# A two-layer trunk on one core: the MLP's down projection as seven block products, with block sums on GpSimd

## The chip, the cores and the metric

One core of a Trainium2 chip runs the whole kernel. The time is that of the device, in microseconds (us), from one launch; lower is better. Engines: TensorE (PE; its weight loads are PEld), VectorE (DVE), ScalarE (ACT), GpSimd (POOL), SyncE (SP), which here only issues DMAs.

## The reference

Two layers over x of 512 tokens by 1024 features, all in float32. Each layer has a token mixer (dilated attention, a gating unit and retention, between an input and an output projection), cross-attention into 256 memory tokens, and an MLP; each of the three has a norm before it and one behind it. Cut to the MLP, and to what is around it:

```python
for l in range(DEPTH):
    ...
    mem_n = rms_norm(mem, g[6])
    x = x + rms_norm(memory_attention(rms_norm(x, g[2]), mem_n, x_wq[l], x_wkv[l], x_wo[l]), g[3])
    h = rms_norm(x, g[4])
    f = jnp.square(jax.nn.relu(h @ w_up[l])) @ w_down[l]     # (512,1024)@(1024,4096), (512,4096)@(4096,1024)
    x = x + rms_norm(f, g[5])
```

## The kernel before

Every float32 product is made of three matmuls in the type fp32r: each operand is split into a high part, rounded, and a low part, the remainder, and hi·hi, hi·lo and lo·hi are summed in PSUM (`three_passes`, L558 to L560). Weights come in blocks of 512 rows by 512 columns, in SBUF as 128 partitions x 2048. A block goes through four steps: SyncE loads it into one of two slots of `w_raw`, ScalarE writes `w_hi` (`split_hi`, L934), VectorE writes `w_lo` = `w_raw` - `w_hi` (`split_lo`, L1193), TensorE uses it. `w_hi` and `w_lo` have two slots as well, so ScalarE may split block b only when TensorE is done with b-2 (semaphore `tile_done`), and SyncE may load only when the slot's block is split (`w_lo_done`).

A layer has 36 head blocks (JOBS), and then the MLP in four groups of 1024 hidden features. A group has eight blocks: `up0`, `up1` (each two blocks of 512 input features) and `dn0`, `dn1` (each two blocks of 512 hidden features). TensorE runs a block as four tiles of 12 matmuls (4 slices of 128 by 3 passes), one tile to each of the four PSUM banks of `proj`. Behind an up tile ScalarE makes the relu (L1114) and the high part `uT_hi` (L1117), VectorE the square (L1487) and the low part `uT_lo` (L1491). Behind the second block of a down job VectorE adds each bank to `ys` (L1500). `ys` was zeroed by GpSimd before (L1644), which does nothing else in the MLP until the norm at the end of the layer.

The order of every engine is written out by hand, each in its own program of straight code and `Fori` loops: an instruction that waits holds up everything behind it on its engine. Around the MLP:

- The third norm (`n3`), between the output of cross-attention and the first up blocks, has its order in two lists, `N3_ACT` and `N3_DVE`. In them e is a tile's square sum or gain, x the updated row tile and its squares, n the norm, h the split of its transposes (L961, L1254), w the split of up block 0 or 1.
- In the last group of a layer the sums of squares of `ys`, the gains (L1238) and the updates of `xs` (L1246) follow the additions of `dn1`, tile by tile; GpSimd takes the roots (L1577, L1579). In layer 0 the memory for the next layer is normed and transposed in the same group, and the next layer's first weight block is loaded when it ends.
- The prologue: SyncE loads positions, a table, the memory tokens `hs`, the gains, the first weight block and x; VectorE makes the angles of the rotary positions (11 small steps); ScalarE loads its sine table, makes sine and cosine, loads the exponential's table (L922 to L925), and only then squares the memory tokens (L1122). GpSimd makes the root, VectorE the norm (L1224), TensorE transposes (L587), and both split the transposes (`memT_hi`, `memT_lo`).

## Time and profile before

| | us |
|---|---|
| median of 3 runs (1556.33 to 1559.43) | 1556.99 |
| the profiled execution, whole | 1556.43 |
| its span (first to last instruction of the trace) | 1554.4 |
| TensorE busy, 8016 matmuls | 1519.2 |
| VectorE busy | 735.9 |
| ScalarE busy | 572.5 |
| GpSimd busy | 177.2 |

The profiled execution's own time is 2.0 us longer than its span. Busy time is the time in which an engine had an instruction in work; matmuls overlap each other in the pipeline, so their mean durations (0.39 us) are longer than the distance from one to the next. The granted clock of TensorE is 0.998 of full over the span. Reading such a profile starts from the engine that is never idle; what the others do counts only where it ends a wait of that one.

### The profile page before, as it was taken

Reading aid. Unit: us, or ns where it says so; the run is one execution under the profiler, and the core shown is the slowest. Engines: PE = TensorE matmul, PEld = TensorE weight load, DVE = VectorE, ACT = ScalarE, POOL = GpSimd, SP = SyncE. Lnnn points to the kernel's source line nnn. Section 1 sums busy time; section 2 is a strip of 40 time slices with the busy share of each in tenths; the row PEclk is TensorE's granted clock in tenths of the full one; section 3 lists DMA queues with packets and bytes.
Section 4 is the critical chain, followed back from the end, with each engine's and each line's share of the span. In section 5 each row is a group of like instructions: output and inputs, shape, how many; then the busy total and the mean of one; then the engine's idle time right before and its main releaser. Section 6 shows DMA issues by size and latency. Waiting matters only on the chain.

```text
span 1554.4 us, 19807 instructions
## 1 busy us (share of the span) xinstructions
PE 1519.2 (98%) x8016; PEld 1302.3 (84%) x8016; DVE 735.9 (47%) x933; ACT 572.5 (37%) x865; POOL 177.2 (11%) x192
## 2 busy tenths in 40 slices
PE   5999999999999999999999999999999999999997
PEld 5978898888888888888898888888888888888886
DVE  5345555724554343433572465755346433444345
ACT  5335434534443232313352453344334423232231
POOL 2001710200110000000040037111003000000001
PEclk9999999999999999999999999999999999999999
DMA  7333132430223332333343232125112232323231
GB/s 248 117 101 102 42 109 82 163 109 28 60 84 106 105 99 91 97 126 115 109 130 115 64 106 91 66 82 175 70 49 88 82 98 92 108 82 108 83 121 55
DMA packets 78991, 153.62 MB, mean 99 GB/s; under 512 B 3520, under 2 KB 19648, under 8 KB 78912
## 3 DMA queue, kind: packets, MB, share of 16 engines
q1 hardware_dynamic: 77904, 150.50, 29.4%
...
q14 instruction: 21, 0.17, 0.0%
...
## 4 chain that ended last, share of the span: by engine, by line
PE 94%; DVE 3%; ACT 1%; issue 1%; POOL 1%; DMA 1%; POOLq 0%; ACTq 0%; SPq 0%; DVEq 0%
PE proj L558 28%; PE proj L560 27%; PE proj L559 27%; PE work L758 2%; PE work L587 2%; PE work L737 2%; PE work L623 1%; PE work L634 1%; PE work L613 1%; DVE w_lo L1193 1%; PE work L712 1%; ACT w_hi L934 0%; DMA w_raw<-in_x_wkv_dram 0%; PE work L691 0%; PE work L745 0%
## 5 line engine op out<-in xcount | busy, mean ns | idle before, releaser
L1193 DVE TENSOR_TENSOR w_lo<-w_raw,w_hi 128x2048 fp32r<-128x2048 f32 (+1 forms) x136 | 297.3, 2186 | 463.7 <-ACT w_hi L934 463.6
L934 ACT ACTIVATE w_hi<-w_raw 128x2048 fp32r<-128x2048 f32 (+1 forms) x136 | 248.2, 1825 | 475.2 <-PE proj L560 469.9
L558 PE MATMUL proj<-hT_hi,w_hi 128*128 128x512 f32 (+1 forms) x800 | 299.3, 374 | 4.3 <-DVE w_lo L1193 4.3
L559 PE MATMUL proj<-hT_lo,w_hi 128*128 128x512 f32 (+1 forms) x800 | 298.2, 373 | 0.0
L560 PE MATMUL proj<-hT_hi,w_lo 128*128 128x512 f32 (+1 forms) x800 | 298.2, 373 | 0.0
L558 PE MATMUL proj<-w_hi,hT_hi 128*128 128x512 f32 (+1 forms) x640 | 238.4, 372 | 1.2 <-DVE hT_lo L1298 1.2
L560 PE MATMUL proj<-w_hi,hT_lo 128*128 128x512 f32 (+1 forms) x640 | 232.2, 363 | 0.0
L559 PE MATMUL proj<-w_lo,hT_hi 128*128 128x512 f32 (+1 forms) x640 | 231.8, 362 | 0.0
L558 PE MATMUL proj<-w_hi,uT_hi 128*128 128x512 f32 x512 | 199.4, 389 | 0.0
L560 PE MATMUL proj<-w_hi,uT_lo 128*128 128x512 f32 x512 | 199.2, 389 | 0.0
L559 PE MATMUL proj<-w_lo,uT_hi 128*128 128x512 f32 x512 | 199.2, 389 | 0.0
L558 PEld LDWEIGHTS proj<-hT_hi,w_hi 128*128 128x128 f32 x800 | 151.2, 189 | 30.9 <-DVE w_lo L1193 4.7
L559 PEld LDWEIGHTS proj<-hT_lo,w_hi 128*128 128x128 f32 x800 | 151.2, 189 | 26.2
L560 PEld LDWEIGHTS proj<-hT_hi,w_lo 128*128 128x128 f32 x800 | 151.2, 189 | 26.0
L558 PEld LDWEIGHTS proj<-w_hi,hT_hi 128*128 128x128 f32 x640 | 120.6, 188 | 13.8 <-DVE hT_lo L1298 1.7
L560 PEld LDWEIGHTS proj<-w_hi,hT_lo 128*128 128x128 f32 x640 | 120.1, 188 | 13.0
L559 PEld LDWEIGHTS proj<-w_lo,hT_hi 128*128 128x128 f32 x640 | 120.4, 188 | 11.8
L559 PEld LDWEIGHTS proj<-w_lo,uT_hi 128*128 128x128 f32 x512 | 96.1, 188 | 20.0
L560 PEld LDWEIGHTS proj<-w_hi,uT_lo 128*128 128x128 f32 x512 | 96.1, 188 | 19.9
L558 PEld LDWEIGHTS proj<-w_hi,uT_hi 128*128 128x128 f32 x512 | 96.1, 188 | 19.9
L1571 POOL TENSOR_SCALAR half_mean<-half_sum 128x4 f32<-128x4 f32 x6 | 1.4, 233 | 908.1 <-ACT half_squares L948 908.1
L1500 DVE TENSOR_TENSOR ys<-proj,ys 128x512 f32<-128x512 f32 x64 | 44.0, 689 | 70.9 <-PE proj L560 70.7
...
## 6 DMA issues: line engine op xcount, KB each, us to landing
w_raw<-in_w_up_dram SPq DMA_DIRECT2D x32, 1024.0 KB, 5.8
w_raw<-in_w_down_dram SPq DMA_DIRECT2D x32, 1024.0 KB, 5.1
...
w_raw<-in_x_wkv_dram SPq DMA_DIRECT2D x16, 1024.0 KB, 5.1
w_raw<-in_w_out_dram SPq DMA_DIRECT2D x8, 1024.0 KB, 5.2
w_raw<-in_x_wq_dram SPq DMA_DIRECT2D x8, 1024.0 KB, 5.1
w_raw<-in_x_wo_dram SPq DMA_DIRECT2D x8, 1024.0 KB, 5.1
gains<-in_norm_g_dram SPq DMA_DIRECT2D x13, 512.0 KB, 6.2
```

The source lines that it names most:

```text
L558: nc.tensor.matmul(dst, l_hi, r_hi, start=first, stop=False)
L559: nc.tensor.matmul(dst, l_hi, r_lo, start=False, stop=False)
L560: return nc.tensor.matmul(dst, l_lo, r_hi, start=False, stop=last)
L587: mm = nc.tensor.transpose(work[:, 2 * (n % 2) + half, k * P:(k + 1) * P], src[:, c * P:(c + 1) * P], ident[:])
L613: mm = nc.tensor.matmul(work[:, head, 0:n], left[rows, p, q], right[rows, p, 0:n], start=i == 0, stop=i == len(passes) - 1)
L623: mm = nc.tensor.transpose(work[:, 2, j * P:(j + 1) * P], probs[:, u % 2, j * P:(j + 1) * P], ident[:])
L634: mm = nc.tensor.matmul(work[HD * head:HD * (head + 1), 3, p * P:(p + 1) * P], va[:, j, (h + head) * HD:(h + head + 1) * HD], probsT[:, he ...
L737: mm = nc.tensor.matmul(work[:, u % 2, i * MEM:(i + 1) * MEM], qxT[:, c, t * P:(t + 1) * P], kmT[:, c, :], start=(k == 0), stop=(k == 1))
L758: mm = nc.tensor.matmul(work[:, 3, k * P:(k + 1) * P], vm[:, j, (pair * BK + k) * P:(pair * BK + k + 1) * P], x_probsT[:, u % 2, (i * MT + ...
L934: nc.scalar.activation(w_hi[:, slot, :, 0:cols], w_raw[:, slot, :, 0:cols], ACT.Copy).then_inc(w_hi_done, 1)
L1193: nc.vector.tensor_tensor(w_lo[:, slot, :, 0:cols], w_raw[:, slot, :, 0:cols], w_hi[:, slot, :, 0:cols].bitcast(F32), ALU.subtract).then_i ...
L1500: nc.vector.tensor_tensor(part_y, proj[:, t], part_y, ALU.add).then_inc(added, 1)
```

## The change

The down projection of a group is a product of A, 512 tokens by 1024 hidden features, and B, 1024 by 1024. Both are cut in four: a11, a12, a21, a22 (first or second 256 tokens, first or second 512 hidden features) and b11 to b22. In place of the eight block products there are seven (Winograd's form of Strassen's scheme), each of 256 tokens by one block of 128x2048, 24 matmuls, on operands that are in part sums:

| product | rows | weights |
|---|---|---|
| m1 | a11 | b11 |
| m2 | a12 | b21 |
| m6 | a21 + a22 - a11 | b22 - b12 + b11 |
| m5 | s1 = a21 + a22 | b12 - b11 |
| m7 | s3 = a11 - a21 | t3 = b22 - b12 |
| m3 | a12 - (a21 + a22 - a11) | b22 |
| m4 | a22 | b21 - (b22 - b12 + b11) |

GpSimd makes the sums in place: four of weights (128x2048 each), s3 (128x1024), s1 and the new a11 in two halves each (128x512), and the new a12 (128x1024). ScalarE and VectorE split the rows of each product (128x1024, three slots `a_hi`, `a_lo`) and its weights (128x2048, the two slots as before). m1, m6, m7 and m4 run in PSUM banks 2 and 3 and stay there as a running sum, m2, m5 and m3 in banks 0 and 1, m3 on top of m5; after every product VectorE adds its two banks to a quarter of `ys` (in the first group it copies four of the seven). The relu is written once to `u` and squared there in place; the split of the up tiles (`uT_hi`, `uT_lo`) is gone, as are the zeroing of `ys` and the loops: each group is written out. Two of four down blocks, b12 and b22, are loaded into new slots (`w_more`) ahead of their group; the bytes loaded are the same.

Beside that: the third norm splits up block 1 before row tile 2 or 3 is squared or updated; the next layer's first two weight blocks are loaded and split in the last group, where only one was; the prologue loads the memory first, in separate semaphores by tile, its gains by ScalarE's queue, the first weight block in halves, and two weight blocks instead of one, and it makes the angles, sine and cosine behind the splits of the memory's transposes.

In the diff below, blank lines and these parts are left out: the new names and semaphores, `load_up` and `load_down`, `product_hi` and `rows_hi` (a split that waits for its operand's sum and for the slot), `add_product`, and what only follows from these.

```diff
-GROUP_JOBS = ("up0", "up1", "dn0", "dn1")
-GROUP_BLOCKS = KB * len(GROUP_JOBS)
+UP_BLOCKS = 2 * KB
+PRODUCTS = ("m1", "m2", "m6", "m5", "m7", "m3", "m4")
+GROUP_BLOCKS = UP_BLOCKS + len(PRODUCTS)
 BLOCKS = HEAD_BLOCKS + GROUPS * GROUP_BLOCKS
+RAW_GROUP = UP_BLOCKS + 2
+RAWS = HEAD_BLOCKS + GROUPS * RAW_GROUP
+ADDS = 2 * len(PRODUCTS)
+ASLOTS = 3
...
-N3_ACT = steps("e0 e1 x0 x1 w0 h0 e2 h1 x2 e3 w1 x3 h2 h3")
-N3_DVE = steps("e0 x0 e1 x1 n0 n1 w0 h0 h1 e2 x2 e3 x3 w1 n2 n3 h2 h3")
+N3_ACT = steps("e0 e1 x0 x1 w0 h0 e2 h1 e3 w1 x2 x3 h2 h3")
+N3_DVE = steps("e0 x0 e1 x1 n0 n1 w0 h0 h1 e2 x2 e3 w1 x3 n2 n3 h2 h3")
...
+        u = part("u", 0, [P, KC, S])
+        s1 = part("s1", 16, [P, BK, S // 2])
+        a_hi = part("a_hi", 20, [P, ASLOTS, BK, S // 2], F32R)
+        a_lo = part("a_lo", 20 + 4 * ASLOTS, [P, ASLOTS, BK, S // 2], F32R)
+        w_more = part("w_more", 44, [P, 3, BK, 512])
+        s3 = nc.alloc_sbuf_tensor_at("s3", [P, BK, S // 2], F32, offset=sgu_start)
+        a11, a21 = u[:, 0:BK, 0:S // 2], u[:, 0:BK, S // 2:S]
+        a12, a22 = u[:, BK:KC, 0:S // 2], u[:, BK:KC, S // 2:S]
+        ROWS = {"m1": a11, "m2": a12, "m6": a11, "m5": s1[:], "m7": s3[:], "m3": a12, "m4": a22}
+        RAW = {"m1": w_raw[:, 0], "m2": w_raw[:, 1], "m6": w_raw[:, 0], "m5": w_more[:, 1], "m7": w_more[:, 2],
+               "m3": w_more[:, 0], "m4": w_raw[:, 1]}
...
+            def free_raws(l, g):
+                sp.wait_ge(w_lo_done, nth(w_lo_done, l, product_block(g, "m6") + 1))
+                sp.wait_ge(t_made, nth(t_made, l, 4 * g + 4))
+            def load_group(l, g):
+                if g:
+                    free_raws(l, g - 1)
+                    load_up(l, g, 0)
+                    sp.wait_ge(w_lo_done, nth(w_lo_done, l, product_block(g - 1, "m5") + 1))
+                    load_down(l, g, w_more[:, 1], 0, 1, q_loaded[1])
+                    sp.wait_ge(w_lo_done, nth(w_lo_done, l, product_block(g - 1, "m3") + 1))
+                    load_down(l, g, w_more[:, 0], 1, 1, q_loaded[0])
+                    sp.wait_ge(w_lo_done, nth(w_lo_done, l, product_block(g - 1, "m4") + 1))
+                    load_up(l, g, 1)
+                else:
+                    for i in range(KB):
+                        sp.wait_ge(w_lo_done, nth(w_lo_done, l, HEAD_BLOCKS - WSLOTS + i + 1))
+                        load_up(l, g, i)
+                    sp.wait_ge(x_weighed, nth(x_weighed, l, XUNITS))
+                    load_down(l, g, w_more[:, 1], 0, 1, q_loaded[1])
+                    load_down(l, g, w_more[:, 0], 1, 1, q_loaded[0])
+                for i in range(KB):
+                    sp.wait_ge(w_lo_done, nth(w_lo_done, l, group_block(g, i) + 1))
+                    load_up(l, g, KB + i)
+                for i in range(KB):
+                    sp.wait_ge(w_lo_done, nth(w_lo_done, l, group_block(g, KB + i) + 1))
+                    load_down(l, g, w_raw[:, i], i, 0, w_loaded[i])
...
-            for dst, src in ((pos_i, positions), (inv, c_inv)):
-                sp.dma_start(dst[:], src).then_inc(first_loaded, 16)
             for t in range(MT):
-                sp.dma_start(hs[:, t], mem[0, t * P:(t + 1) * P]).then_inc(mem_loaded, 16)
-            load_gain(0, "mem")
-            load_block(PROLOGUE, BLOCKS, x_wkv[0:1, 0:BK * P, 0:512])
-            for t in range(T):
+                sp.dma_start(hs[:, t], mem[0, t * P:(t + 1) * P]).then_inc(mem_first[t], 16)
+            for h in range(2):
+                k = BK // 2 * h
+                sp.dma_start(w_raw[:, 0, k:k + BK // 2],
+                             x_wkv[0, k * P:(k + BK // 2) * P, 0:512].rearrange("(k p) c -> p k c", p=P)).then_inc(w_first[h], 16)
+            load_block(PROLOGUE, BLOCKS + 1, x_wkv[0:1, BK * P:2 * BK * P, 0:512])
+            sp.dma_start(xs[:, 0], x[0, 0:P]).then_inc(x_loaded[0], 16)
+            load_gain(0, "n1")
+            for t in range(1, T):
                 sp.dma_start(xs[:, t], x[0, t * P:(t + 1) * P]).then_inc(x_loaded[t], 16)
+            start_counts(sp, mem_loaded)
+            sp.sem_inc(w_loaded[0], 16)
...
+            def product(l, g, name):
+                n = PRODUCTS.index(name)
+                b = product_block(g, name)
+                a = (len(PRODUCTS) * g + n) % ASLOTS
+                bank = 2 if name in ("m1", "m6", "m7", "m4") else 0
+                fresh = name in ("m1", "m2", "m5")
+                pe.wait_ge(w_lo_done, nth(w_lo_done, l, b + 1))
+                pe.wait_ge(a_lo_done, nth(a_lo_done, l, len(PRODUCTS) * g + n + 1))
+                for i in range(2):
+                    if name == "m1":
+                        pe.wait_ge(relued, nth(relued, l, UP_TILES * g + 6 + i + 1))
+                    elif n >= 2:
+                        pe.wait_ge(added, nth(added, l, ADDS * g + 2 * (n - 2) + i + 1))
+                    rows = slice(i * P, (i + 1) * P)
+                    for k in range(BK):
+                        mm = three_passes(proj[:, bank + i], a_hi[:, a, k, rows], a_lo[:, a, k, rows],
+                                          w_hi[:, b % WSLOTS, k], w_lo[:, b % WSLOTS, k],
+                                          fresh and k == 0, k == BK - 1, more=True)
+                    mm.then_inc(tile_done, 1)
+                    if name == "m3" and g == GROUPS - 1 and l < DEPTH - 1:
+                        turn_normed(l, "memk", i)
...
+            def mlp_group(l, g):
+                last = g == GROUPS - 1
+                if g:
+                    split_hi(l, group_block(g, 1))
+                split_hi(l, group_block(g, 2))
+                if last and l < DEPTH - 1:
+                    act.wait_ge(turned, nth(turned, l, 2 * TURNED["n3", T - 1] + 2))
+                    for t in range(MT):
+                        act.dma_start(hs[:, t], mem[0, t * P:(t + 1) * P]).then_inc(mem_loaded, 16)
+                    act.dma_start(gains[:, GAIN_SLOT["mem"]],
+                                  norm_g[l + 1:l + 2, GAIN["mem"]].broadcast_to([P, D])).then_inc(gain_loaded["mem"], 16)
+                for m in range(4):
+                    relu_up(l, g, m)
+                split_hi(l, group_block(g, 3))
+                rows_hi(l, g, "m1")
+                product_hi(l, g, "m1")
+                for m in range(4, 8):
+                    relu_up(l, g, m)
+                product_hi(l, g, "m2")
+                rows_hi(l, g, "m2")
+                rows_hi(l, g, "m6")
+                product_hi(l, g, "m6")
+                rows_hi(l, g, "m5")
+                product_hi(l, g, "m5")
+                rows_hi(l, g, "m7")
+                if last:
+                    e3_squares(l, 0, (0, 1))
+                product_hi(l, g, "m7")
+                rows_hi(l, g, "m3")
+                product_hi(l, g, "m3")
+                rows_hi(l, g, "m4")
+                product_hi(l, g, "m4")
+                if not last:
+                    split_hi(l, group_block(g + 1, 0))
+                    return
+                e3_squares(l, 0, (2, 3))
+                if l < DEPTH - 1:
+                    split_hi(l, BLOCKS)
+                    for t in range(MT):
+                        turn_hi(l, ("memk", t), memT_hi, t)
+                e3_squares(l, 1, (0, 1))
+                if l < DEPTH - 1:
+                    split_hi(l, BLOCKS + 1)
+                e3_squares(l, 1, (2, 3))
...
+            def mlp_group(l, g):
+                last = g == GROUPS - 1
+                if g:
+                    split_lo(l, group_block(g, 1))
+                split_lo(l, group_block(g, 2))
+                for m in range(4):
+                    square_up(l, g, m)
+                split_lo(l, group_block(g, 3))
+                rows_lo(l, g, "m1")
+                if last and l < DEPTH - 1:
+                    for t in range(MT):
+                        norm_mem(l, "memk", t)
+                product_lo(l, g, "m1")
+                for m in range(4, 8):
+                    square_up(l, g, m)
+                product_lo(l, g, "m2")
+                rows_lo(l, g, "m2")
+                for n, name in enumerate(PRODUCTS[:-2]):
+                    add_product(l, g, name, 0)
+                    add_product(l, g, name, 1)
+                    rows_lo(l, g, PRODUCTS[n + 2])
+                    product_lo(l, g, PRODUCTS[n + 2])
+                add_product(l, g, "m3", 0)
+                if last:
+                    gain(l, "e3", 0, 0)
+                    gain(l, "e3", 0, 1)
+                add_product(l, g, "m3", 1)
+                if not last:
+                    split_lo(l, group_block(g + 1, 0))
+                    add_product(l, g, "m4", 0)
+                    add_product(l, g, "m4", 1)
+                    return
+                if l < DEPTH - 1:
+                    split_lo(l, BLOCKS)
+                    for t in range(MT):
+                        turn_lo(l, ("memk", t), memT_hi, memT_lo, t)
+                gain(l, "e3", 0, 2)
+                gain(l, "e3", 0, 3)
+                gain(l, "e3", 1, 0)
+                update(l, "e3", 0)
+                add_product(l, g, "m4", 0)
+                add_product(l, g, "m4", 1)
+                if l < DEPTH - 1:
+                    split_lo(l, BLOCKS + 1)
+                gain(l, "e3", 1, 1)
+                update(l, "e3", 1)
+                for t in (2, 3):
+                    gain(l, "e3", 1, t)
+                    update(l, "e3", t)
...
+            def mlp_group(l, g):
+                b11, b21 = w_raw[:, 0], w_raw[:, 1]
+                b22, b12, t3 = w_more[:, 0], w_more[:, 1], w_more[:, 2]
+                def rows_read(name):
+                    pool.wait_ge(a_lo_done, nth(a_lo_done, l, len(PRODUCTS) * g + PRODUCTS.index(name) + 1))
+                for q in q_loaded:
+                    pool.wait_ge(q, nth(q, l, 16 * (g + 1)))
+                if g:
+                    pool.wait_ge(w_lo_done, nth(w_lo_done, l, product_block(g - 1, "m7") + 1))
+                else:
+                    pool.wait_ge(x_weighed, nth(x_weighed, l, XUNITS))
+                nc.gpsimd.tensor_tensor(t3, b22, b12, ALU.subtract).then_inc(t_made, 1)
+                r = HEAD_BLOCKS + RAW_GROUP * g + UP_BLOCKS
+                pool.wait_ge(w_loaded[0], nth(w_loaded[0], l, 16 * (r // WSLOTS + 1)))
+                pool.wait_ge(t_made, nth(t_made, l, 4 * g + 1))
+                nc.gpsimd.tensor_tensor(b12, b12, b11, ALU.subtract).then_inc(t_made, 1)
+                pool.wait_ge(hidden, nth(hidden, l, UP_TILES * g + BK))
+                if g:
+                    pool.wait_ge(a_lo_done, nth(a_lo_done, l, len(PRODUCTS) * (g - 1) + PRODUCTS.index("m7") + 1))
+                nc.gpsimd.tensor_tensor(s3[:], a11, a21, ALU.subtract).then_inc(s_made, 1)
+                pool.wait_ge(w_lo_done, nth(w_lo_done, l, product_block(g, "m1") + 1))
+                pool.wait_ge(t_made, nth(t_made, l, 4 * g + 2))
+                nc.gpsimd.tensor_tensor(b11, t3, b11, ALU.add).then_inc(t_made, 1)
+                rows_read("m1")
+                for half in range(2):
+                    k = slice(half * 2, half * 2 + 2)
+                    pool.wait_ge(hidden, nth(hidden, l, UP_TILES * g + BK + half * 2 + 2))
+                    nc.gpsimd.tensor_tensor(s1[:, k], a21[:, k], a22[:, k], ALU.add).then_inc(s_made, 1)
+                    pool.wait_ge(s_made, nth(s_made, l, 6 * g + 2 * half + 2))
+                    nc.gpsimd.tensor_tensor(a11[:, k], s1[:, k], a11[:, k], ALU.subtract).then_inc(s_made, 1)
+                pool.wait_ge(w_lo_done, nth(w_lo_done, l, product_block(g, "m2") + 1))
+                pool.wait_ge(t_made, nth(t_made, l, 4 * g + 3))
+                nc.gpsimd.tensor_tensor(b21, b21, b11, ALU.subtract).then_inc(t_made, 1)
+                rows_read("m2")
+                pool.wait_ge(s_made, nth(s_made, l, 6 * g + 5))
+                nc.gpsimd.tensor_tensor(a12, a12, a11, ALU.subtract).then_inc(s_made, 1)
...
-                nc.gpsimd.memset(ys[:], 0.0).then_inc(y_zeroed, 1)
+                for g in range(GROUPS):
+                    mlp_group(l, g)
```

## Rows read from the trace of the kernel before

**Rows 1.** the page: busy time, and the chain that ended last
```profile
PE 1519.2 (98%) x8016; PEld 1302.3 (84%) x8016; DVE 735.9 (47%) x933; ACT 572.5 (37%) x865; POOL 177.2 (11%) x192
...
PE 94%; DVE 3%; ACT 1%; issue 1%; POOL 1%; DMA 1%; POOLq 0%; ACTq 0%; SPq 0%; DVEq 0%
```

**Rows 2.** TensorE's waits: us in total, times, longest us
```profile
PE work L587 <- DVE hs L1224: 13.9, 1, 13.9
PE proj L558 <- DVE w_lo L1193: 7.6, 4, 2.2
```

**Rows 3.** windows, one middle group (busy PE, PEld, DVE, ACT, POOL)
```profile
578.85:665.89 87.04, 87.04 (x386) 72.07 (x385) 34.04 (x33) 24.27 (x24) 0.00 (x0) 1.00 0.30 97
```

**Rows 4.** timeline of an up block: start us, us, engine, line, operation
```profile
533.70 0.39 PE L558 MATMUL proj<-hT_hi,w_hi 128*128 128x512 f32 x1
...
533.98 0.60 ACT L1114 ACTIVATE relu<-proj 128x512 f32<-128x512 f32 x1 [0.89 <-PE proj L560]
...
537.33 0.69 DVE L1487 TENSOR_TENSOR relu<-relu 128x512 f32<-128x512 f32 x1 [1.31 <-ACT relu L1114]
```

**Rows 5.** the line of w_lo (ns min/median/max), then groups by form (mean ns)
```profile
L1193 DVE TENSOR_TENSOR w_lo<-w_raw,w_hi x136: 1757/2291/2294, 14.9 to 1527.8; 128x2048 fp32r<-128x2048 f32 x108, 128x1536 fp32r<-128x1536 f32 x28
...
L1209 DVE SCALAR_TENSOR_TENSOR hs<-xs,rstd,gains 128x1024 f32<-128x1024 f32 x24 | 30.8, 1283 | 8.7 <-POOL rstd L1566 8.7
...
L934 ACT ACTIVATE w_hi<-w_raw 128x2048 fp32r<-128x2048 f32 x108 | 206.6, 1913 | 436.9 <-PE proj L560 431.7 <-DMA w_raw<-in_x_wkv_dram 5.1
```

**Rows 6.** groups by form, GpSimd
```profile
L1594 POOL TENSOR_TENSOR qkc<-rot 128x384 f32<-128x384 f32 x8 | 8.3, 1039 | 0.6
...
L1619 POOL TENSOR_TENSOR vs<-vs,ln_gain 128x1024 f32<-128x1024 f32 x2 | 4.8, 2400 | 12.2 <-DVE vs L1313 12.2
```

**Rows 7.** timeline, GpSimd beside VectorE, two places
```profile
141.83 2.37 POOL L1621 TENSOR_TENSOR vs<-vs,ln_shift 128x1024 f32<-128x1024 f32 x1
...
142.00 2.35 DVE L1262 TENSOR_SCALAR probs<-probs,rden 128x256 f32<-128x256 f32 x1
...
938.60 1.08 POOL L1594 TENSOR_TENSOR qkc<-rot 128x384 f32<-128x384 f32 x1
939.64 2.53 POOL L1595 TENSOR_TENSOR qkc<-qkc,rot 128x384 f32<-128x384 f32 x1
...
939.23 2.06 DVE L1193 TENSOR_TENSOR w_lo<-w_raw,w_hi 128x1536 fp32r<-128x1536 f32 x1 [0.42 <-ACT w_hi L934]
```

**Rows 8.** timeline, a handover near the kernel's end
```profile
1547.70 1.28 DVE L1246 SCALAR_TENSOR_TENSOR xs<-ys,rstd,xs 128x1024 f32<-128x1024 f32 x1
1548.90 0.68 DVE L1238 TENSOR_TENSOR ys<-ys,gains 128x512 f32<-128x512 f32 x1
...
1547.83 1.20 POOL L1577 TENSOR_TENSOR meansq<-sumsq,half_mean 128x1 f32<-128x1 f32 x1 [0.89 <-ACT squares L954]
```

**Rows 9.** DMA issues: engine op xcount, KB each, us to landing
```profile
w_raw<-in_w_down_dram SPq DMA_DIRECT2D x32, 1024.0 KB, 5.1
...
gains<-in_norm_g_dram SPq DMA_DIRECT2D x13, 512.0 KB, 6.2
```

**Rows 10.** timeline of the prologue, and the last update
```profile
9.07 1.04 ACT L1122 ACTIVATE squares<-hs 128x1024 bf16<-128x1024 f32 x1
11.59 1.91 ACT L934 ACTIVATE w_hi<-w_raw 128x2048 fp32r<-128x2048 f32 x1 [0.35 <-DMA w_raw<-in_x_wkv_dram]
...
12.47 2.48 DVE L1224 SCALAR_TENSOR_TENSOR hs<-hs,mem_rstd,gains 128x1024 f32<-128x1024 f32 x2 [5.42 <-POOL mem_rstd L1604]
...
19.59 0.39 PE L558 MATMUL proj<-memT_hi,w_hi 128*128 128x256 f32 x1 [2.05 <-DVE memT_lo L1254]
...
1550.03 1.28 DVE L1246 SCALAR_TENSOR_TENSOR xs<-ys,rstd,xs 128x1024 f32<-128x1024 f32 x1 [0.44 <-POOL rstd L1579]
```

**Rows 11.** window behind the first pause, and eight later transposes on the timeline
```profile
13.90:15.00 1.10, 1.10 (x6) 1.10 (x7) 1.10 (x2) 0.00 (x0) 0.00 (x0) 1.00 1.04 413
...
437.23 1.03 PE L587 MATMUL work<-ident,hs 128*128 128x128 f32 x8
```

415 lines of the change are left out of this document (215 added, 200 removed).

## The prediction, made before the changed kernel ran

> **What bounds the kernel now.** I read the page first: TensorE is busy for 98% of the span, and the chain that ended last is TensorE for 94% [rows 1]. The list of waits then shows how little can be won by waiting less: TensorE waits 13.9 us once at the start and 7.6 us in four waits for w_lo; these two lines lead the list [rows 2]. One middle MLP group of eight blocks, by windows, takes 87.04 us with TensorE busy throughout, VectorE for 34.0 us, GpSimd not at all [rows 3]: a block of 48 matmuls lasts 10.88 us, a tile of 12 lasts 2.72 us. So the MLP is bound by the number of matmuls, and everything the change adds to other engines is free until it makes TensorE wait. The timeline gives the delays: ScalarE starts 0.28 us after the next tile's first matmul; a relu lasts 0.60 us, a square 0.69 us [rows 4].
>
> **What goes.** A group has four down blocks of 48 matmuls; afterwards it has seven products of 24. 24 matmuls fewer are 5.44 us, over 8 groups **-43.5 us**. A group without waits would last 81.6 us. The memset of ys (GpSimd, unwaited for) goes at no gain.
>
> **What comes.** Each product still needs a whole split of a 128x2048 block (ScalarE 1.91, VectorE 2.29 us by the median) [rows 5], but TensorE spends only 5.44 us on it, and with two slots the split may start only when the product two before is done. VectorE has per product that split, a 128x1024 remainder (1.28 us by the nearest row; between the 512 and 2048 forms it would be 1.2, which I take) and two additions of 0.69: 4.9 of 5.44 us. ScalarE has 1.91 + 1.05 (the 128x1024 form, [rows 10]). That fits, barely, if nothing else holds VectorE up.
>
> GpSimd comes in per group with four sums of 128x2048 and the equal of four of 128x1024. It has a two-input 1024 form at 2.40 us and a 384 form at 1.04 [rows 6]: 2.13 ns an element, so 4.6, 2.4 and 1.27 us for 2048, 1024 and 512. There is no row of 2048; in proportion to the 1024 form it would be 4.8, so I take 4.2 to 5.0 as ends. The walk below holds two such sums in series: 0.8 us of wait a group either way, 6 us in all.
> The Trainium skill (GPSIMD Engine Reference, Elementwise — side-by-side cycle accounting) has 4497 ns for a two-input sum of 2048; by it the time would be about 2 us less.
>
> **The port.** A VectorE subtraction with both inputs in SBUF began beside a GpSimd operation and lasted 2.06 us, where its form, the shorter on that line, takes 1.76 at the least [rows 5, 7]; the next GpSimd operation of 384 elements lasted 2.53 us instead of 1.0, that is, until the subtraction had ended. A VectorE scaling of 256 elements begun 0.17 us into a 2.37 us GpSimd operation lasted 2.35 us [rows 7]. So each waits for the other's whole instruction. When both are ready at the end of an instruction the one that waited longer goes first: GpSimd's small sum of 1547.83 ended 0.13 us after the next VectorE instruction's start, not behind it [rows 8]. By these rows a handover comes 0.14 us ahead of the record's end.
> The Trainium skill says the same (SBUF — State Buffer, Who interferes with whom): a VectorE instruction with two SBUF inputs and a GpSimd one that reads SBUF exclude each other for a whole instruction. It speaks against this change, and the trace agrees.
>
> **One group on that port**, in us from the start of m1 on TensorE (the end of the last up block):
> - w_lo of m1 until -6.4, square 4 until -5.8; then the sum into b11, -6.0 to -1.3. Squares 5 and 6, ready at -4.5 and -1.9, wait: done -0.8 and -0.2.
> - First halves of the two row sums and square 7, in turn: -0.3 to 1.0, 0.9 to 1.6, 1.5 to 2.8.
> - w_hi of m2 comes behind relu 7 (0.9 to 2.7), w_lo 2.7 to 5.0; the second s1 half, waiting, takes 4.9 to 6.2, the remainder of m2's rows 6.0 to 7.25. m1 ended at 5.44: **wait 1.85 us**; m2 ends 12.7.
> - Second a11 half 7.1 to 8.4; from it ScalarE makes m6's rows until 9.5. But GpSimd is free at once for the 4.6 us sum into b21 (8.5 to 13.1), needed only by the last product. Behind it m6's row remainder 13.0 to 14.1, then, waiting longer, the sum into a12 until 16.4, then w_lo of m6 until 18.55. m6 starts 18.6 instead of 12.7: **wait 5.85 us**.
> - From there VectorE's 4.9 us fit into each 5.44.
>
> That is 7.7 us a group, **+61.6 us**. At six seams between groups the next t3 sum (its data issued after m3's split, 5.1 us to landing [rows 9]) ends about 0.2 us too late for the first up block's w_lo: +1.2. The sum into b12, s3 and their loads lie in the up phase, where a block lasts 10.88 us and its split 4.2; 4.6 us more still fit, so they cost nothing.
>
> **The rest.** Prologue: ScalarE sits behind sine and exponential tables until 9.07, the norm starts at 12.47, the first product at 19.59 [rows 10]. Memory is now loaded first, the tables come later, and the gains are issued near 1.0 on ScalarE's queue; with the 6.2 us to landing of such a load [rows 9] the norm starts near 7.2. The first weight block, whose load ended at 11.59, is issued 1.5 us earlier and in halves: near 10. Its two small splits and the four remainders of memT (0.6 each) then end near 14.5: -5.0, and one of the four w_lo waits (1.9 in the mean) goes: **-6.9** (ends -3 and -8.5). Behind it the eleven trigonometric steps, 3 us on VectorE, stand before the second split; the first block's 5.7 us cover them, without that cover they'd cost 3. Third norm: two waits of up to 2.2 us for w_lo go, the transposes' remainders are late next, so I take half of 2 x 2.2: **-2.2**. Layer seam: the w_lo wait goes, but VectorE now puts one split, four remainders, three gains and an update (some 9 us) ahead of the last product's additions, on whose banks the next block waits: 0 (ends -1.9, +2). Tail: m4's additions stand behind one update of 1.28 and gains; the last update, 1550.03 now [rows 10], ends later by **+1.6** (ends 0, +3).
>
> **Sum**: -43.5 +61.6 +1.2 -6.9 -2.2 +1.6 = +11.8 on the profiled execution's 1556.4 us (span 1554.4): 1568.2; against the runs' median of 1557.0, 0.6 higher, **1569**. The wait per group at which the change earns nothing is 49.8 / 8 = 6.2 us. A measurement tells 0.2%, 3 us, from no change.
>
> **Rivals.**
> - *VectorE keeps the port* over instructions that follow one another. Then the waits are 0.7 and 4.95, 5.65 in all, and the time 1552. Rows 8 speak against it; its rows are of tiny sums.
> - *The port's queue is shorter* than I walked it: if the sum into b11 ends before square 5 is ready, the second a11 half ends at 4.3, not 8.4, and about 2.7 us a group are left: 1529, **faster**. For it: each start hangs on margins of 0.1 to 0.5 us. Against: the sum can't start before w_lo of m1.
> - *No exclusion for subtractions*: rows 7 have only 0.30 us of it on one. Then 0.7 us a group: 1512.
> - *The clock*. After the first 13.9 us pause six transposes stand in 1.10 us, 0.18 each; later eight stand in 1.03, 0.13 each, though the granted clock reads 1.00, the 2.4 GHz level, in both [rows 11]. If the product behind each 5.85 us pause runs slower, at most 5.44 us, at half that 2.7 a group: 1591. Against: the granted clock, and that each product is followed at once by three or more without a pause.
> The Trainium skill (TensorE: Matmul & The Clock Gate, Rules for kernel authors) says that idle gaps of this length bring the half rate back; no row here shows a granted clock below 1.00.
> - *It doesn't do what it says*: 192 matmuls remain, 1600. Nothing speaks for it.
>
> **Chances.** As walked 0.42 (own range 1558 to 1580), VectorE keeps the port 0.14, shorter queue 0.18, no exclusion 0.12, clock 0.12, not as it says 0.02. Faster: 0.18 + 0.12 + 0.08 of the 0.14 = 0.38; same 0.05; slower 0.57. The range takes in the shorter queue and most of the clock's case, 1524 to 1592; no exclusion stays outside.
>
> **What would show it.** TensorE waiting in every group for m2's row remainder (about 1.9 us) and m6's w_lo (about 5.9), and nowhere else in the MLP; L1193-like subtractions of over 4 us beside GpSimd's sums; GpSimd busy 28 us a group or more; the first matmul before 10 us. Wrong, if those subtractions all last 2.29 us, if waits per group are under 6.2 us, or if the 2048 sums last well under 4.2.

## The result, and the profile after

The changed kernel takes 1606.41 us (median of 4 runs, 1605.50 to 1607.57) against 1556.66 for the kernel before (4 runs, 1555.93 to 1559.43): a ratio of 1.0317, 95% interval 1.0299 to 1.0334. It is slower, as forecast, but by 50 us and not by 12, and it lies 14 us above the range of 1524 to 1592. Its span is 1604.1 us.

The page of the profile, busy time and chain, as in [rows 1]:
```profile
PE 1506.9 (94%) x7824; PEld 1283.3 (80%) x7824; DVE 971.9 (61%) x998; ACT 636.5 (40%) x883; POOL 453.7 (28%) x272
...
PE 81%; DVE 9%; POOL 5%; ACT 2%; issue 2%; DMA 1%; SPq 0%; DVEq 0%; POOLq 0%; ACTq 0%
```
The 192 matmuls are gone, and TensorE is busy 12 us less, not 43.5: matmuls became longer. It now idles for 6% of the span. Its waits (us in total, times, longest):
```profile
PE proj L647 <- DVE w_lo L1333: 43.0, 8, 5.4
PE proj L647 <- DVE a_lo L1340: 13.6, 8, 1.7
PE work L676 <- DVE hs L1378: 12.8, 5, 4.0
PE work L676 <- DMA ident<-in_c_ident_dram: 9.0, 1, 9.0
```
The first two lines are one wait ahead of m6 and one ahead of m2 in each of the eight groups. The third is new too: two in each layer's third norm, one at the layer seam. What makes m6 late is seen in one middle group on the timeline, GpSimd first, then VectorE, then TensorE:
```profile
578.03 4.65 POOL L1831 TENSOR_TENSOR w_raw<-w_raw 128x2048 f32<-128x2048 f32 x1
582.61 3.36 POOL L1835 TENSOR_TENSOR u<-u 128x1024 f32<-128x1024 f32 x1
...
579.20 4.56 DVE L1340 TENSOR_TENSOR a_lo<-u,a_hi 128x1024 fp32r<-128x1024 f32 x1 [1.08 <-ACT a_hi L1058]
583.68 4.43 DVE L1333 TENSOR_TENSOR w_lo<-w_raw,w_hi 128x2048 fp32r<-128x2048 f32 x1
...
577.07 0.47 PE L647 MATMUL proj<-w_hi,a_hi 128*128 128x512 f32 x1 [1.70 <-DVE a_lo L1340]
588.17 0.80 PE L647 MATMUL proj<-w_hi,a_hi 128*128 128x512 f32 x1 [5.41 <-DVE w_lo L1333]
588.76 0.63 PE L648 MATMUL proj<-w_lo,a_hi 128*128 128x512 f32 x1
589.19 0.63 PE L649 MATMUL proj<-w_hi,a_lo 128*128 128x512 f32 x1
...
593.43 0.40 PE L647 MATMUL proj<-w_hi,a_hi 128*128 128x512 f32 x1
593.67 0.40 PE L648 MATMUL proj<-w_lo,a_hi 128*128 128x512 f32 x1
```
The sum for m4 (L1831), needed last of all, holds m6's row remainder up until 582.7; the remainder's record, 4.56 us for 1.2 us of work, is mostly waiting. Then the sum for m3 (L1835) holds up the remainder of m6's weights. That is the walk of the forecast to within half a microsecond. What it did not have is in the last lines: from 588.17 on matmuls start 0.43 us apart in place of 0.23, until 593.4. The windows of that stretch (the third figure from the end is the granted clock), the group's 26 us ahead of the pause among them:
```profile
556.00:582.00 26.00, 24.30 (x108) 19.85 (x107) 18.00 (x11) 10.87 (x10) 18.05 (x7) 1.00 0.10 38
588.00:593.00 5.00, 4.83 (x11) 3.80 (x12) 4.65 (x5) 0.00 (x0) 0.00 (x0) 0.50 0.65 209
546.75:638.85 92.10, 84.84 (x362) 69.02 (x360) 62.51 (x41) 32.39 (x26) 35.26 (x11) 0.96 0.28 92
```
Granted clock 0.50, the 1.2 GHz level, behind the pause of 5.41 us; 1.00 behind m2's of 1.70. The twelve distances from 588.17 to 593.43 take 5.26 us; the same twelve behind m2's wait take 2.81. That is 2.45 us in this group. Over the eight groups, ten to twelve matmuls are slow each time. The whole group, from one sum into b12 to the next, takes 92.10 us where [rows 3] had 87.04.

**Where the 49.7 us of span are.** I took the same instruction in both traces at six places; what the shift gains between two of them belongs to that stretch:

| stretch | forecast | found |
|---|---|---|
| prologue (first kmT, 31.82 and 28.08) | -6.9 | -3.7 |
| third norm (first relu of the MLP, 451.05 and 452.08; in layer 1 1215.94 and 1244.92) | -2.2 | +7.3 (4.8 and 2.5; in layer 1 the kernel before lost some itself) |
| eight groups | +19.3 | +39.5 |
| layer seam | 0 | +5.0 |
| behind the last matmul (1545.88 and 1594.00, ends of span) | +1.6 | +1.6 |
| sum | +11.8 | +49.7 |

The third norm in layer 0, GpSimd, VectorE and TensorE:
```profile
432.46 4.55 POOL L1806 TENSOR_TENSOR w_more<-w_more 128x2048 f32<-128x2048 f32 x1
...
432.53 5.56 DVE L1378 SCALAR_TENSOR_TENSOR hs<-xs,rstd,gains 128x1024 f32<-128x1024 f32 x1 [0.72 <-PE work L676]
...
438.15 1.97 PE L676 MATMUL work<-ident,hs 128*128 128x128 f32 x8 [3.76 <-DVE hs L1378]
```
GpSimd's first block sum t3 starts 0.07 us ahead of the last norm, which then lasts 5.56 us in place of 1.28. TensorE waits 3.76 us and runs its next transposes slowly (granted clock 0.66 from 436 to 446). Layer 1 has the same wait, at 1231.73.

### The profile page after: what moved, and what is told of

Its sections match the earlier page's. It is cut to its first block, busy times and chain, and to the rows that moved or that the text cites. A ratio compares the mean times of both kernels' runs of the same rounds, so it can differ in the third digit from the quotient of the medians.

```text
span 1604.1 us, 19050 instructions
## 1 busy us (share of the span) xinstructions
PE 1506.9 (94%) x7824; PEld 1283.3 (80%) x7824; DVE 971.9 (61%) x998; ACT 636.5 (40%) x883; POOL 453.7 (28%) x272
## 4 chain that ended last, share of the span: by engine, by line
PE 81%; DVE 9%; POOL 5%; ACT 2%; issue 2%; DMA 1%; SPq 0%; DVEq 0%; POOLq 0%; ACTq 0%
PE proj L647 23%; PE proj L649 23%; PE proj L648 23%; POOL s L1825 2%; DVE w_lo L1333 2%; DVE u L1346 2%; POOL u L1827 2%; PE work L676 2%; PE work L847 2%; DVE w_lo L1326 2%; PE work L826 2%; PE work L712 1%; PE work L723 1%; ACT w_hi L1032 1%; PE work L702 1%
## 5 line engine op out<-in xcount | busy, mean ns | idle before, releaser
L1326 DVE TENSOR_TENSOR w_lo<-w_raw,w_hi 128x2048 fp32r<-128x2048 f32 (+1 forms) x103 | 229.0, 2224 | 287.6 <-ACT w_hi L1032 287.3
L1032 ACT ACTIVATE w_hi<-w_raw 128x2048 fp32r<-128x2048 f32 (+1 forms) x103 | 185.1, 1797 | 245.7 <-PE proj L649 244.7
L647 PE MATMUL proj<-w_hi,a_hi 128*128 128x512 f32 x448 | 184.1, 411 | 56.6 <-DVE w_lo L1333 43.0
L648 PE MATMUL proj<-w_lo,a_hi 128*128 128x512 f32 x448 | 181.6, 405 | 0.0
L649 PE MATMUL proj<-w_hi,a_lo 128*128 128x512 f32 x448 | 181.1, 404 | 0.0
L647 PEld LDWEIGHTS proj<-w_hi,a_hi 128*128 128x128 f32 x448 | 89.0, 199 | 81.8 <-DVE w_lo L1333 46.4
L648 PEld LDWEIGHTS proj<-w_lo,hT_hi 128*128 128x128 f32 x640 | 120.4, 188 | 11.8
L1346 DVE TENSOR_TENSOR u<-u 128x512 f32<-128x512 f32 x64 | 84.1, 1329 | 49.2 <-ACT u L1223 49.2
L1340 DVE TENSOR_TENSOR a_lo<-u,a_hi 128x1024 fp32r<-128x1024 f32 x40 | 106.0, 2651 | 8.6 <-ACT a_hi L1058 8.6
L1333 DVE TENSOR_TENSOR w_lo<-w_raw,w_hi 128x2048 fp32r<-128x2048 f32 x32 | 90.5, 2828 | 33.7 <-ACT w_hi L1046 33.7
L649 PEld LDWEIGHTS proj<-w_hi,a_lo 128*128 128x128 f32 x448 | 88.4, 197 | 19.4
```

The source lines that it names most:

```text
L647: nc.tensor.matmul(dst, l_hi, r_hi, start=first, stop=False, skip_group_check=more)
L648: nc.tensor.matmul(dst, l_hi, r_lo, start=False, stop=False, skip_group_check=more)
L649: return nc.tensor.matmul(dst, l_lo, r_hi, start=False, stop=last, skip_group_check=more)
L1032: nc.scalar.activation(w_hi[:, slot, :, 0:cols], w_raw[:, raw, :, 0:cols], ACT.Copy).then_inc(w_hi_done, 1)
L1326: nc.vector.tensor_tensor(w_lo[:, slot, :, 0:cols], w_raw[:, raw, :, 0:cols], w_hi[:, slot, :, 0:cols].bitcast(F32), ALU.subtract).then_in ...
L1333: nc.vector.tensor_tensor(w_lo[:, b % WSLOTS], RAW[name], w_hi[:, b % WSLOTS].bitcast(F32), ALU.subtract).then_inc(w_lo_done, 1)
```

## Experiments

Two theories to start with. *Port and order*: TensorE waits because VectorE's instructions with two SBUF inputs and GpSimd's sums exclude each other, and the two sums L1831 and L1835 come at the worst moment; then the half clock behind the pause. *Engine time*: GpSimd or the chain through it is simply too slow, whatever VectorE does. Runs e1 to e4 are single runs, beside 1556.16 for the kernel before; e5 to e7 stand beside a median of 1556.77, e8 to e10 beside 1556.41. A span is that of the one profiled execution and can lie 2 us from the span of the median run, so small differences are read from the medians.

**e1: both late sums only behind m6's split.**
```diff
-                pool.wait_ge(w_lo_done, nth(w_lo_done, l, product_block(g, "m2") + 1))
+                pool.wait_ge(w_lo_done, nth(w_lo_done, l, product_block(g, "m6") + 1))
+                rows_read("m2")
+                nc.gpsimd.tensor_tensor(a12, a12, a11, ALU.subtract).then_inc(s_made, 1)
                 nc.gpsimd.tensor_tensor(b21, b21, b11, ALU.subtract).then_inc(t_made, 1)
-                rows_read("m2")
-                nc.gpsimd.tensor_tensor(a12, a12, a11, ALU.subtract).then_inc(s_made, 1)
```


> Edit: GpSimd makes the a12 sum and then the b21 sum only behind m6's w_lo, instead of ahead of it. Theory (port and clock: a GpSimd sum holds the port that VectorE's subtractions need, and a pause of over 5 us halves TensorE's rate behind it): the wait for m6's w_lo falls from 5.4 to about 1 us a group, but VectorE has only 0.5 us free per product, so the 7 us of sums now stand before m5's or m7's w_lo and some 5 us of wait a group appear there; time 1575 to 1606. Rival (VectorE is simply full, GpSimd is not the cause): the wait stays before m6, time unchanged at 1606. Rival (m6's operands are late because the GpSimd chain itself is long): wait at m6 gone, none elsewhere, 1545.

1603.33 us, span 1601.5. TensorE's waits in one middle group (556 to 648):
```profile
PE proj L647 <- DVE w_lo L1333: 4.9, 2, 4.4
PE proj L647 <- DVE a_lo L1340: 1.7, 1, 1.7
```
and on VectorE in that group:
```profile
584.78 6.65 DVE L1333 TENSOR_TENSOR w_lo<-w_more,w_hi 128x2048 fp32r<-128x2048 f32 x1
```
The pause moved from m6 to m5 (0.56 and 4.38 us in place of 5.41), with half the rate behind it as before, and the time is inside the 1575 to 1606 expected. Delaying whole sums only hands the wait on. A GpSimd chain that is merely long would have left no other wait, and 1545.

**e2: the same GpSimd time without reading.** Each sum is replaced by writes to the same place of about the same length.
```diff
-                nc.gpsimd.tensor_tensor(b21, b21, b11, ALU.subtract).then_inc(t_made, 1)
+                write_sum(b21, t_made)
```
`write_sum` is two memsets of the whole range and one of half of it, one behind the other; all sums are replaced in this way and so are not computed.

> Edit: every GpSimd sum is replaced by writes of constants to the same places that last as long (2.5 memsets of the same size), with the same waits; the sums are left out of the computation. Theory (port: only GpSimd's reads shut VectorE out): VectorE's subtractions fall back to 2.29 us, waits in a group fall from 7.1 us to 1 or less, the granted clock goes back to 1.00 in the MLP, 1510 to 1520. Rival (the length of the GpSimd chain): GpSimd is as busy as before, so waits and time stay, 1595 to 1606. Rival (VectorE is full): the same, 1606.

1518.33 us, span 1516.5. The page's busy time, and VectorE on one product beside it:
```profile
PE 1480.2 (98%) x7824; PEld 1267.1 (84%) x7824; DVE 842.0 (56%) x998; ACT 636.3 (42%) x883; POOL 398.4 (26%) x432
...
566.23 1.22 DVE L1341 TENSOR_TENSOR a_lo<-s,a_hi 128x1024 fp32r<-128x1024 f32 x1
567.64 2.29 DVE L1334 TENSOR_TENSOR w_lo<-w_more,w_hi 128x2048 fp32r<-128x2048 f32 x1 [0.19 <-ACT w_hi L1047]
```
GpSimd is busy for 398 us (454 with the sums, which hold waiting as well), and no subtraction is longer than its own 2.29 or 1.22 us: the wait for w_lo in the products is gone altogether. What VectorE waits for is GpSimd's reading, not GpSimd's time. Engine time as the cause falls.

**e3: one sum taken out.** The sum for m4 reads and writes one column of each slice of 512; m4's weights are left unsummed else.
```diff
-                nc.gpsimd.tensor_tensor(b21, b21, b11, ALU.subtract).then_inc(t_made, 1)
+                nc.gpsimd.tensor_tensor(b21[:, :, 0:1], b21[:, :, 0:1], b11[:, :, 0:1], ALU.subtract).then_inc(t_made, 1)
```


> Edit: the b21 sum covers one column of each slice instead of 512, so m4 is computed with wrong weights; all else as it is. Theory: m6's w_lo waits only for the a12 sum, about 2 us instead of 5.4, and a pause so short leaves the clock up: 3.4 + 3.3 us a group less, about 1552. Rival (VectorE is full): 1606. Rival (clock has another cause than the pause): 3.4 us a group, 1579.

1554.41 us, span 1552.6; in one group:
```profile
PE proj L647 <- DVE a_lo L1340: 1.7, 1, 1.7
PE proj L647 <- DVE w_lo L1333: 1.2, 1, 1.2
```
4.6 us less on the port are 4.2 us less wait a group, 34 us in all. The clock gives the rest of the 51.5 saved: with the pause at 1.2 us the granted clock of a group is 1.00, and by the starts in the trace the eight products behind it take 18.4 us less.

**e4: the pause filled.** 22 matmuls of 512 columns into unused banks of `work`, directly ahead of m6; nothing else changes.
```diff
+                if name == "m6":
+                    for i in range(22):
+                        nc.tensor.matmul(work[:, 2 + i % 2], hT_hi[:, i % KC, 0:P], hT_lo[:, (i + 1) % KC], start=True, stop=True)
```


> Edit: ahead of m6 TensorE runs 22 matmuls of 512 columns into unused banks, 5 us, so it does not idle while m6's w_lo is made; nothing else changes. Theory (the pause lowers TensorE's rate, 3.3 us a group): the granted clock stays at 1.00 in m6, wait at m6 about 0.4 us, 8 x 3.3 = 26 us less, about 1580. Rival (m6 is slow for another reason, such as the first use of a12 or bank conflicts with VectorE's additions): no gain, 1606.

1589.77 us, span 1588.0: faster by 16.1 us of span for 176 matmuls more. TensorE in a middle group:
```profile
580.02 0.39 PE L650 MATMUL proj<-w_hi,a_lo 128*128 128x512 f32 x1
580.25 5.15 PE L957 MATMUL work<-hT_lo,hT_hi 128*128 128x512 f32 x22
585.84 0.50 PE L648 MATMUL proj<-w_hi,a_hi 128*128 128x512 f32 x1 [0.44 <-DVE w_lo L1337]
586.17 0.39 PE L649 MATMUL proj<-w_lo,a_hi 128*128 128x512 f32 x1
586.40 0.40 PE L650 MATMUL proj<-w_hi,a_lo 128*128 128x512 f32 x1
```
m6 starts 5.82 us behind the last start of m2, as in the changed kernel (5.80), but at full rate from its first matmul. So it is the idling that slows m6 down, and not m6's operands or banks. The gain is 16 us and not the 26 expected (3.3 a group): the eight products are 2.0 to 2.5 us shorter, 18.6 in all, and a part came back as waits elsewhere (in the group shown the one for the next up block's split grew from 0.15 to 0.35 us).

**e5: t3 behind the last norm.**
```diff
                     pool.wait_ge(x_weighed, nth(x_weighed, l, XUNITS))
+                    pool.wait_ge(normed, nth(normed, l, NORMED["n3", T - 1] + 1))
```


> Theory: the third norm got slower (4.8 us a layer later at the first MLP relu, where the forecast had 2.2 us earlier) because GpSimd's first block sum (line 1806) starts with the last norm (line 1378) and holds it for 5.56 us in place of 1.28; TensorE then waits 3.76 us and runs its next products at half rate. This kernel holds that sum back until the last norm of the third is made. Expected: the longest wait of TensorE for hs in that stretch gone (from 12.8 us in 5 to about 5), the clock at 1.00 there, 5 to 7 us in each of the two layers, so a span of 1590 to 1594 against 1604.1. Rival: the norm was late anyway, because its squares and the root came late; then the span stays within 3 us of 1604.

1595.06 us (1592.76 to 1596.42), ratio to before 1.0242 (1.0225 to 1.0259), span 1594.6. The norm's line, and the window over the third norm:
```profile
L1378 DVE SCALAR_TENSOR_TENSOR hs<-xs,rstd,gains x24: 1274/1284/1286, 23.3 to 1220.5; 128x1024 f32<-128x1024 f32 x24
...
400.00:470.00 70.00, 69.36 (x414) 61.66 (x413) 43.57 (x34) 28.11 (x40) 28.27 (x21) 1.00 0.31 106
```
No norm is over 1286 ns and the clock stays at 1.00. The span is 9.5 us shorter, 0.6 us outside the range expected; the medians differ by 11.4. In the two third norms themselves, from the same instructions as in the table, 11.8 us are saved, 6.2 and 5.5. One moved wait removes the whole loss of that stretch; the rival falls.

**e6: the order in the products.** On e5; all work stays.
```diff
-                rows_hi(l, g, "m6")
                 product_hi(l, g, "m6")
+                rows_hi(l, g, "m6")
...
-                    rows_lo(l, g, PRODUCTS[n + 2])
-                    product_lo(l, g, PRODUCTS[n + 2])
+                    if n == 0:
+                        product_lo(l, g, "m6")
+                        rows_lo(l, g, "m6")
+                        rows_lo(l, g, "m5")
+                    elif n == 1:
+                        product_lo(l, g, "m5")
+                        rows_lo(l, g, "m7")
+                    elif n == 2:
+                        product_lo(l, g, "m7")
...
+                    if half:
+                        rows_read("m2")
                     nc.gpsimd.tensor_tensor(a11[:, k], s1[:, k], a11[:, k], ALU.subtract).then_inc(s_made, 1)
...
-                pool.wait_ge(w_lo_done, nth(w_lo_done, l, product_block(g, "m2") + 1))
-                nc.gpsimd.tensor_tensor(b21, b21, b11, ALU.subtract).then_inc(t_made, 1)
-                rows_read("m2")
+                rows_read("m5")
+                nc.gpsimd.tensor_tensor(b21[:, 0:2], b21[:, 0:2], b11[:, 0:2], ALU.subtract)
+                rows_read("m7")
+                nc.gpsimd.tensor_tensor(b21[:, 2:4], b21[:, 2:4], b11[:, 2:4], ALU.subtract).then_inc(t_made, 1)
+                pool.wait_ge(w_lo_done, nth(w_lo_done, l, product_block(g, "m7") + 1))
                 nc.gpsimd.tensor_tensor(a12, a12, a11, ALU.subtract).then_inc(s_made, 1)
```


> On top of the run before, the order in a group is changed and no work is taken away: on ScalarE and VectorE the split of m6's weights goes ahead of its rows, GpSimd makes the second half of a11's sum only when VectorE has made m2's a_lo, and its sums for m4 and m3 (lines 1831 and 1835) come after m5's and m7's splits, the first in two halves. Theory (the read port is exclusive, and the loss is one of order): VectorE and GpSimd together need the port for about 38 us of the 38 us of the seven products, so order can take out most of the 5.4 us pause ahead of m6, with the 2.4 us of half rate behind it; what stays is 1 to 3 us a group. Expected: 8 x (5 to 7) us below the run before, a span of 1535 to 1552. Rival (sheer port time: it only moves, as when the b21 sum alone was moved): the pause turns up ahead of m5, m7 or m4, and the span is above 1575.

1554.61 us (10 runs, 1552.23 to 1556.96), ratio 0.9985 (0.9976 to 0.9995), span 1554.5: 40 us gone by order alone (one sum is made in two pieces); the span is 2.5 us above what the theory expected and 20 under the rival's bound. TensorE's waits:
```profile
PE proj L647 <- DVE w_lo L1333: 14.6, 8, 1.9
PE proj L647 <- DVE a_lo L1340: 13.9, 8, 2.1
PE work L676 <- DVE hs L1393: 9.3, 2, 8.9
PE work L676 <- DVE hs L1378: 5.2, 3, 3.9
PE proj L647 <- DVE w_lo L1326: 4.1, 5, 0.9
```
43.0 us became 14.6, but these 1.9 us a group sit ahead of m3, whose sum now comes too late, and the waits in the up phase are 4.1 us in place of 1.3. With m2's wait, left as it was, that is 4.1 us a group where 1 to 3 were expected.

**e7: one sum out of the products.** On e6; in three of four groups t3 + b11 goes into the norms' buffer `hs`, free then, during the up projection.
```diff
+        b11_sum = hs[:].rearrange("p a (b c) -> p (a b) c", c=512)
...
+                if g < GROUPS - 1:
+                    nc.gpsimd.tensor_tensor(b11_sum, t3, b11, ALU.add).then_inc(t_made, 1)
```


> As the run before, and the sum b11 + t3 is written to the room of the norm's buffer hs in three of four groups, so that GpSimd makes it during the up projection, when VectorE has little to do, and not between the squares and m2's splits (line 1819, 5.0 us, now starts with the split of m1). Theory of port time: 4.6 us of it leave the products, the squares of lines 1346 are free of it, and m2's a_lo comes earlier: 0.8 to 2 us a group less waiting ahead of m2 and m6 than in the run before in six of eight groups, 5 to 12 us in all, a span of 1525 to 1545. Rival: what bounds there is the chain relu, square, sum, split, and not the port: within 3 us of the run before.

1551.51 us (1550.48 to 1553.25), ratio 0.9970 (0.9957 to 0.9982), span 1548.9. The profiled spans differ by 5.6 us, but the medians by 3.1: less than the 5 to 12 expected and at the rival's bound of 3, so this run alone does not tell the two apart, though the waits moved as the theory has it. m2's wait fell from 1.7 to 0.73 us in the four middle groups; ahead of m3 TensorE still waited 1.84 to 1.98. Twice that brought half the rate for some eight matmuls (behind the wait that ended at 675.08, starts 0.43 us apart from 676.35 on), while the same 1.98 us at 588.88 brought none.

**e8: two sums moved once more.** On e7.
```diff
-                    pool.wait_ge(w_lo_done, nth(w_lo_done, l, product_block(g - 1, "m7") + 1))
+                    pool.wait_ge(w_lo_done, nth(w_lo_done, l, group_block(g, 1) + 1))
...
                 rows_read("m7")
-                nc.gpsimd.tensor_tensor(b21[:, 2:4], b21[:, 2:4], b11[:, 2:4], ALU.subtract).then_inc(t_made, 1)
+                nc.gpsimd.tensor_tensor(a12, a12, a11, ALU.subtract).then_inc(s_made, 1)
                 pool.wait_ge(w_lo_done, nth(w_lo_done, l, product_block(g, "m7") + 1))
-                nc.gpsimd.tensor_tensor(a12, a12, a11, ALU.subtract).then_inc(s_made, 1)
+                nc.gpsimd.tensor_tensor(b21[:, 2:4], b21[:, 2:4], b11[:, 2:4], ALU.subtract).then_inc(t_made, 1)
```


> As the run before (e7), with two of GpSimd's sums moved once more, no work added or left out: the sum for m3 (line 1864 there) goes ahead of the second half of the sum for m4, since TensorE waited 1.98 us for m3 in each group; and the next group's first sum (line 1824 there) starts only behind the first two splits of the up projection, one of which took 4.28 us in place of 2.29 beside it, with a wait of 0.95. Theory of port and order: both waits go, 2.4 to 2.9 us in each of eight groups, and the 2 us of half rate that the pause of 1.98 brought in the second group shown, so 18 to 30 us: a span of 1519 to 1531 against 1548.9. Rival: the order only passes the wait on to m7 or m4, and the span stays above 1540.

1527.26 us (1525.93 to 1528.47), ratio 0.9812 (0.9799 to 0.9826), span 1526.2, inside the range. The list of waits has no w_lo of the MLP any more. What each of the two moves gave was not run apart.

**e9: squares on ScalarE.** On e8.
```diff
                 nc.scalar.activation(u[:, m], proj[:, m % 4], ACT.Relu).then_inc(relued, 1)
+                if m < UP_TILES - 1:
+                    act.wait_ge(relued, nth(relued, l, UP_TILES * g + m + 1))
+                    nc.scalar.activation(u[:, m], u[:, m], ACT.Square).then_inc(hidden, 1)
```


> As e8, and ScalarE makes seven of the eight squares of a group (lines 1346 of the kernel after; 0.69 us of port time each on VectorE), the last stays on VectorE. Theory: in e7 they held the port only in the up projection, where nothing waited for it, and the last square still sets m2's rows: no more than 3 us in all, a span within 3 us of e8. Rival (port time is short everywhere): 0.7 us a group and more, at least 6 us below e8.

1523.59 us (1522.23 to 1524.59), ratio 0.9788 (0.9775 to 0.9801), span 1522.4, 3.8 us below e8: between the two theories. The wait for a_lo fell from 9.8 to 5.8 us, but not evenly: in the first and last group of a layer from 1.6 to 1.9 us to 0.73, in the middle ones not at all. So the squares delayed m2's rows in half of the groups only. Waits, a window around one group, and GpSimd over that group and into the next:
```profile
PE proj L652 <- DVE a_lo L1350: 5.8, 8, 0.7
...
534.00:620.00 86.00, 85.23 (x375) 69.83 (x374) 50.28 (x34) 39.95 (x36) 34.74 (x13) 1.00 0.28 98
```
```profile
515.98 4.60 POOL L1824 TENSOR_TENSOR w_more<-w_more 128x2048 f32<-128x2048 f32 x1 [19.06 <-DVE w_lo L1336]
...
567.12 2.41 POOL L1858 TENSOR_TENSOR w_raw<-w_raw,hs 128x1024 f32<-128x1024 f32 x1 [4.66 <-DVE a_lo L1350]
572.90 2.40 POOL L1861 TENSOR_TENSOR u<-u 128x1024 f32<-128x1024 f32 x1 [3.36 <-DVE a_lo L1350]
577.53 2.41 POOL L1864 TENSOR_TENSOR w_raw<-w_raw,hs 128x1024 f32<-128x1024 f32 x1 [2.23 <-DVE w_lo L1343]
598.98 4.60 POOL L1824 TENSOR_TENSOR w_more<-w_more 128x2048 f32<-128x2048 f32 x1 [19.04 <-DVE w_lo L1336]
```
The late sums each last their own 2.4 us, each released by the VectorE instruction ahead; VectorE's next subtraction is held up by 0.5 to 1.2 us, and TensorE does not wait for it. A group takes 83.0 us (515.98 to 598.98); 81.6 would be TensorE without any wait. This version computes the same products as the changed kernel, and beats both kernels: 33 us under the kernel before, 83 under the changed one.

**e10: the third norm's old order.** On e5.
```diff
-N3_ACT = steps("e0 e1 x0 x1 w0 h0 e2 h1 e3 w1 x2 x3 h2 h3")
+N3_ACT = steps("e0 e1 x0 x1 w0 h0 e2 h1 x2 e3 w1 x3 h2 h3")
-N3_DVE = steps("e0 x0 e1 x1 n0 n1 w0 h0 h1 e2 x2 e3 w1 x3 n2 n3 h2 h3")
+N3_DVE = steps("e0 x0 e1 x1 n0 n1 w0 h0 h1 e2 x2 e3 x3 w1 n2 n3 h2 h3")
```


> The kernel of e5 (the change with the first block sum held back until the last norm) with the third norm's order put back to that of the kernel before, on ScalarE and VectorE. The forecast gave the new order 2.2 us in all (1.1 a layer). Expected by it: 1 to 3 us slower than e5's span of 1594.6. Rival: the new order gains nothing by itself, or loses, since e5 still has its first products behind the same transposes: within 1 us of e5, or below it.

1598.76 us (1597.25 to 1599.76) and span 1596.2: 1.6 us of span and 3.7 of the medians slower than e5, and 4.4 us in the two third norms (2.8 and 1.6), where 1 to 3 were expected. The wait is back on the split that the new order had moved forward:
```profile
PE proj L647 <- DVE w_lo L1326: 5.4, 7, 2.2
```

## Why the prediction was right in direction and wrong in size

- **Fewer matmuls, -43.5**: right. e9 shows it when little else stands in the way: -4.0 us a group and -32 us of span against the kernel before.
- **The port, +61.6**: right, nearly to the number: 1.70 and 5.38 us a group against 1.85 and 5.85, 7.1 against 7.7 (7.4 by the distances between starts). The 2048 sum lasts 4.6 us as estimated (L1831, 4.65). e2 and e3 show that it is the port, e1 that the order decides where the wait falls.
The Trainium skill's rule (SBUF — State Buffer, Who interferes with whom), by which a GpSimd instruction that reads and a VectorE one with two SBUF inputs exclude each other for a whole instruction, agrees with this trace's 4.56 us for a 1.2 us remainder and with e2, where writes alone held nothing up.
- **The clock, priced as a rival at 0.12 and left out of the sum**: this is the step that failed most. "Against: the granted clock, and that each product is followed at once by three or more without a pause": neither argument holds. The granted clock falls to 0.50 behind each pause of 5.4 us, and the product behind it is slow for 5.3 us all the same. The price was 2.7 us a group, found 2.0 to 2.5, 18.6 us in all: most of the 20.2 us that the groups are over the forecast, and half of the whole miss of 37.9 us of span. None of the prediction's signs of being wrong came up, since they asked about the port only. And the trace of before had shown the slow clock. I read the first pause [rows 11], where the granted clock read 1.00 although the transposes were slow, and wrote that no row shows less; the window behind the wait of 2.16 us in layer 1's third norm does:
```profile
1197.00:1206.00 9.00, 6.92 (x46) 6.92 (x47) 6.11 (x6) 3.04 (x6) 5.93 (x3) 0.81 0.36 118
```
That reading spoke for the clock's case, and so for 1591 by the prediction's own price; against it stood the same wait in layer 0, with 1.00 behind it.
The Trainium skill's rule that idle gaps bring the half rate back (TensorE: Matmul & The Clock Gate, Why this matters for your kernels) is borne out by the 0.50 window, and e4 prices it: 16 us for eight pauses, once they are filled.
- **Third norm, -2.2**: the term for the order had the right sign and was rather low (e10: 3.7 us by the medians, 4.4 in the stretch). What failed is the walk of GpSimd: I costed t3 only at "six seams between groups" and not in the first group of a layer, where its wait is the end of cross-attention and its data have long been there, so that it lands on the last norm. That is 9.5 us (+7.3 in place of -2.2), and e5 recovers more than that: 11.8 us in the stretch.
- **Layer seam, 0 with ends -1.9 and +2**: +5.0, outside its ends. TensorE waits 0.43, 0.66 and 3.96 us there; the last for the next layer's first norm:
```profile
815.07 0.69 DVE L1407 TENSOR_TENSOR ys<-ys,gains 128x512 f32<-128x512 f32 x1
815.86 1.28 DVE L1415 SCALAR_TENSOR_TENSOR xs<-ys,rstd,xs 128x1024 f32<-128x1024 f32 x1
817.06 1.28 DVE L1378 SCALAR_TENSOR_TENSOR hs<-xs,rstd,gains 128x1024 f32<-128x1024 f32 x1
```
I costed what stands ahead of the additions on VectorE, and not the norm that stands behind them. VectorE's own queue makes it late: from 799.89 to 818.34 it has no gap over 0.11 us, so it hardly waited for GpSimd's roots. The block sums have no part in it, for in e2, where none reads, the wait is 4.0 us too. Another order there was not run.
- **Prologue, -6.9**: -3.7, inside its ends. The first norm starts at 7.51 us (forecast 7.2), but the second memory tile's only at 10.06, and the first product at 16.23 in place of 14.5:
```profile
16.23 0.38 PE L647 MATMUL proj<-memT_hi,w_hi 128*128 128x256 f32 x1 [2.92 <-DVE memT_lo L1423]
```
It ran at half rate at first (starts 0.21 us apart for 256 columns, 0.12 later). The part was not run alone, so its cause stays open.
- **Tail, +1.6**: found +1.6; no run took it apart.
- The last rival's price was miscounted: with the 192 matmuls kept, the sum's own terms give some 1612, not 1600. Nothing hangs on it, as the page counts 7824.
- The rivals on the fast side fall: the row sums did not catch the shorter queue, VectorE did not keep the port over two instructions (the sum L1835 ran between m6's two remainders), and the exclusion holds for subtractions.
